# A two-layer encoder trunk in split fp32: the high and low parts of the stationary operands laid side by side

## The reference, cut to what matters

```python
for l in range(DEPTH):                                  # DEPTH = 2
    u = x @ (ev_w_in if l % 2 == 0 else od_w_in)[j]     # 2048 -> 6144 (6152) columns
    # layer 0: GLU -> causal depthwise conv (31 taps) -> LayerNorm -> silu | HGRN2, 8 heads, chunks of 64
    # layer 1: forgetting attention, 8 heads | chunked attention with a relative bias, 8 heads
    mix = concatenate([left, right], -1) @ w_out[j]     # 2048 -> 2048
    x = layer_norm(ALPHA * x + mix, ln_mix_g[l], ln_mix_b[l])
    h = square(relu(x @ mlp_w1[l])) @ mlp_w2[l]         # 2048 -> 8192 -> 2048
    x = layer_norm(ALPHA * x + h, ln_mlp_g[l], ln_mlp_b[l])
```

## Time and profile before

| | |
|---|---|
| median of the runs | 2276.03 us (2274.78 to 2277.2) |
| profiled execution | 2273.79 us, of which its span 2272.1 us |
| TensorE matmul busy | 2242.8 us, 99%, 10331 matmuls |
| TensorE weight load busy | 1858.2 us, 82%, 10331 loads |
| VectorE busy | 1341.5 us, 59% |
| ScalarE busy | 1056.6 us, 47% |
| DMA | 418.50 MB, 184 GB/s on average |
| granted TensorE clock | 0.998 of full |

### The profile page before, as it was taken

One profiled execution on the slowest core, in us unless ns is written; L12 is line 12 of the kernel. 1 busy time (PEld: TensorE's weight loads), 2 busy tenths in 40 slices (PEclk: granted clock), 3 DMA queues, 4 the chain that ended last, 5 costly groups with the idle time before them and its releaser, 6 DMA issues.

```text
span 2272.1 us, 28509 instructions
## 1 busy us (share of the span) xinstructions
PE 2242.8 (99%) x10331; PEld 1858.2 (82%) x10331; DVE 1341.5 (59%) x1472; ACT 1056.6 (47%) x1146; POOL 36.3 (2%) x68
## 2 busy tenths in 40 slices
PE   8999999999999999999999999999999999999998
PEld 7888778788888888888878888887888888888886
DVE  4898987855545444545565445568455454544455
ACT  4555565454354344444334444444544444443542
POOL 2000000000000001000000000000000000000000
PEclk9999999999999999999999999999999999999999
DMA  7555545565656656555636555575555565555553
GB/s 243 173 161 157 174 133 180 173 212 188 197 190 224 202 185 203 185 185 187 196 123 191 174 177 166 160 230 170 185 190 185 185 227 198 181 192 200 183 188 111
DMA packets 213040, 418.50 MB, mean 184 GB/s; under 512 B 12793, under 2 KB 13361, under 8 KB 211904
## 3 DMA queue, kind: packets, MB, share of 16 engines
q1 hardware_dynamic: 210832, 406.37, 55.7%
q0 software_dynamic: 1808, 10.04, 1.2%
q10 hardware_dynamic: 288, 0.52, 0.1%
HBM read 414.79 MB, written 2.10 MB: 183 GB/s over the span
## 4 chain that ended last, share of the span: by engine, by line
PE 91%; DVE 5%; issue 1%; ACT 1%; DMA 1%; SPq 0%; POOL 0%; DVEq 0%; ACTq 0%
PE gemm L1349 29%; PE gemm L1351 28%; PE gemm L1350 28%; DVE lnp L1091 1%; PE pair L1735 1%; DVE w_lo L811 1%; PE pair L1504 1%; ACT w_hi L495 1%; DMA raw<-in_ev_w_out 1%; PE pair L1421 1%; PE pair L1461 0%; DMA raw<-in_ev_w_in 0%; PE pair L1577 0%; PE pair L1649 0%; PE pair L1622 0%
## 5 line engine op out<-in xcount | busy, mean ns | idle before, releaser
L1222 DVE TENSOR_TENSOR w_lo<-raw,w_hi 128x1024 fp32r<-128x1024 f32 x488 | 596.7, 1225 | 482.0 <-ACT w_hi L719 452.2
L719 ACT ACTIVATE w_hi<-raw 128x1024 fp32r<-128x1024 f32 x492 | 521.9, 1061 | 629.3 <-PE gemm L1351 608.5
L1349 PE MATMUL gemm<-w_hi,x_hi 128*128 128x512 f32 x1792 | 708.7, 395 | 6.9 <-DVE w_lo L811 5.5
L1351 PE MATMUL gemm<-w_hi,x_lo 128*128 128x512 f32 x1792 | 699.0, 390 | 0.0
L1350 PE MATMUL gemm<-w_lo,x_hi 128*128 128x512 f32 x1792 | 698.3, 390 | 0.0
L1349 PE MATMUL gemm<-w_hi,c_hi 128*128 128x512 f32 x1280 | 501.0, 391 | 1.6 <-DVE X L839 1.0
L1351 PE MATMUL gemm<-w_hi,c_lo 128*128 128x512 f32 x1280 | 498.9, 390 | 0.0
L1350 PE MATMUL gemm<-w_lo,c_hi 128*128 128x512 f32 x1280 | 498.7, 390 | 0.0
L811 DVE TENSOR_TENSOR w_lo<-raw,w_hi 128x1024 fp32r<-128x1024 f32 x280 | 340.4, 1223 | 190.0 <-ACT w_hi L495 184.3
L495 ACT ACTIVATE w_hi<-raw 128x1024 fp32r<-128x1024 f32 x276 | 289.7, 1057 | 304.3 <-PE gemm L1351 266.0
L1349 PEld LDWEIGHTS gemm<-w_hi,x_hi 128*128 128x128 f32 x1792 | 337.0, 188 | 81.7 <-issue 5.4
(11 more groups left out here) (194 smaller groups left out, 798.4 us busy)
## 6 DMA issues: line engine op xcount, KB each, us to landing
raw<-in_mlp_w SPq DMA_DIRECT2D x512, 512.0 KB, 4.7
raw<-in_ev_w_in SPq DMA_DIRECT2D x96, 512.0 KB, 3.8
raw<-in_od_w_in SPq DMA_DIRECT2D x96, 512.0 KB, 4.0
raw<-in_ev_w_out SPq DMA_DIRECT2D x32, 512.0 KB, 4.1
raw<-in_od_w_out SPq DMA_DIRECT2D x32, 512.0 KB, 3.6
lnp<-in_ln_mix_g POOLq DMA_DIRECT2D x2, 1024.0 KB, 6.0
lnp<-in_ln_mix_b POOLq DMA_DIRECT2D x2, 1024.0 KB, 7.7
lnp<-in_ln_mlp_g POOLq DMA_DIRECT2D x2, 1024.0 KB, 7.6
```

The costliest lines, as they stand in the source:

```text
L719: act.activation(hi_of_chunk(s), raw[:, s % RING], ACT.Copy).then_inc(hi_ready, 1)
L1222: dve.tensor_tensor(lo_of_chunk(s), raw[:, s % RING], hi_of_chunk(s).bitcast(F32), ALU.subtract).then_inc(lo_ready, 1)
L1349: pe.matmul(acc[:, r, :], hi[:, k + c, rows], high, start=begin, stop=False)
L1351: return pe.matmul(acc[:, r, :], lo[:, k + c, rows], high, start=False, stop=end)
```

## The change

The two tiles of x become one tile with a last dimension of two, and so do the two of the output tiles' operand. `x_hi`, `x_lo`, `c_hi` and `c_lo` are views of every other element. All that reads or writes them is unchanged in text, and addresses with a step of two elements (8 bytes) where it had a step of one: the stationary operand of every gemm product, the moving operand of lines 1592 to 1594, ScalarE's writes of the high parts, VectorE's reads of the high parts and writes of the low parts. The size in SBUF is the same. The instructions and their order on each engine are the same, and the line numbers behind the change are higher by one.

```diff
-        x_hi = sb("x_hi", [P, KT, S], F32R)
-        x_lo = sb("x_lo", [P, KT, S], F32R)
-        c_hi = sb("c_hi", [P, KT, S], F32R)
-        c_lo = sb("c_lo", [P, KT, S], F32R)
+
+        x_parts = sb("x_parts", [P, KT, S, 2], F32R)
+        c_parts = sb("c_parts", [P, KT, S, 2], F32R)
+        x_hi, x_lo = x_parts[:, :, :, 0], x_parts[:, :, :, 1]
+        c_hi, c_lo = c_parts[:, :, :, 0], c_parts[:, :, :, 1]
```

## The result

The kernel after takes 2332.73 us (2331.57 to 2333.87, three runs) against 2276.03: ratio 1.0249, 95% interval 1.0226 to 1.0272, so 56.7 us slower. Its profiled span is 2331.0 us, 58.9 more than before. The forecast was 2276.2 us, and the range ended at 2298.

The account below looks back on a forecast made before the run. TensorE, 91% of the chain, was taken as the bound, with 9216 matmuls at 0.2267 us. All terms were zero but 0.2 us for ScalarE: 2273.79 + 0.2 = 2274.0, plus 2.2 to the runs' median, 2276.2 us; range 2272 to 2298.

Parts of the forecast that it names:

- (1): Gemm stationary operands: 9216 loads with a step of two stay covered by the 227 ns window; taken as zero.
- Rival B: Loads and the 48 forget-logit streams: the step doubles them, exposed outside the stream; 2296 us, 0.9% slower, chance 0.14.
- 0.21 us between two loads: First two loads behind the transposes: sign of a doubled load, against 0.11 us if unchanged.
- the chain's piece: Eight transposes in the chain, or the gemm after: 0.98 instead of 0.87 us would be a sign of a doubled load.
- a reason, not a proof: Gemm stream: loads take nothing measurable from it today, which doesn't prove that a load over twice the memory wouldn't.
- Rival C: Gemm stream: the load becomes the bound, or collides with the stream; slower by much, chance 0.21.
- C's main case: Gemm loads: interval above 227 ns becomes the bound; with three times the interval +900 us, about 3180 us.
- Its second case: Gemm stream: strided load collides with the moving operand, 13 ns more per matmul, +123 us, 2399 us.
- Step (2): The 48 forget-logit matmuls stream with the step: between zero and +5.1 us; taken as zero.
- (3): ScalarE's 74 writes of high parts: at most 0.09 us each for 1024 elements; 0.2 us taken on the path.
- (4): VectorE's subtractions with the step: zero.
- Step (5): Order, DMAs, semaphores and bytes in SBUF stay as they were: zero.

Follow-up runs that it names:

- one_short: Kernel before, MLP first product: middle of three matmuls streams 64 columns, load step varied by tile; three matmuls take 574 ns at step one, 580 at two.
- pad8: Kernel before with 8 unused elements (32 bytes) in front of x_hi and 120 behind c_lo, no step: 2329.01 us, ratio 1.023.
- blocks: Changed kernel with high and low parts sharing a tile as whole blocks of 256 tokens, without a step: 2275.67 us, ratio 0.9996 to the kernel before.
- pad64: Kernel before with 64 unused elements (256 bytes) in front of x_hi and 64 behind c_lo, no step: 2276.26 us, ratio 0.9999.

## Why the prediction was wrong

**The step that failed is (1), the zero for 9216 strided loads.** It stood for two claims. The first, that the load still fits in its window, held: 118 ns of 227 (`one_short`). Rival B's doubled load fell with it: of its signs, 0.21 us between two loads and 0.98 for the chain's piece, the trace has 0.12 and 0.87. The second, that a strided load leaves the stream's interval as it is, was wrong. With the strided load each interval is 6.6 ns longer, 52.9 us in all. I had argued it away by comparing a matmul that has a load beside it with the last one, which has none. That compares recorded lengths of 0.39 us, which are latencies, while the price sits in the interval: in `pad8` the record grew by 7 ns only together with 233.3. Even the last matmul of the kernel after, with no load beside it, is recorded longer:

```profile
2320.42 0.40 PE L1352 MATMUL gemm<-w_hi,c_parts 128*128 128x512 f32 x1
```

So its record doesn't isolate the load's effect at all. The sentence "a reason, not a proof" was right, and the zero had no better support than that. The row chosen as nearest is of VectorE, which is another reader with no second stream of TensorE beside it.

**Rival C's collision came nearest, at twice the size.** C's main case, a load that becomes the bound, did not occur. Its second case took the 13 ns that the stream has above its 213.3 as the price of a collision and came to 2399 us. Measured were 6.6 ns. Half of those 13 ns would have given 9216 x 6.5 = 60 us, close to the 56.7 measured, but no row supports the half, so that would have been luck. The reason that the prediction gave for a collision, a load spread over twice the memory, isn't the whole of it either: `pad8` pays the same 6.6 ns with loads of neighbouring elements. The prediction asked only about the step and never about the start.

**Step (2) failed in the choice.** The upper end, +5.1 us, was the right one: +5.4 measured. The sixteen matmuls of 64 columns in the earlier trace rows could not show a doubling, as the prediction said of them, and yet I took zero. The Trainium skill, SBUF — State Buffer, section "Door 1: The DMA port swizzle", wants two hits in a 16-byte line for full bandwidth, and a step of two has them. For the moving operand the trace disagrees: single elements and pairs, each with two hits a line, run at half speed (451 ns), and only groups of four are near the full rate (231.1 and 233.3). For the load's own length it nearly agrees: some 6 ns more at step two. It says nothing of load and stream together.

**Steps (3) and (4) held.** ScalarE's line 707 went from 1025 to 1089 ns, inside the bound, and TensorE doesn't wait for it; VectorE's line 1208 stayed at 1224. **Step (5) held**: order and bytes changed nothing, as `blocks` shows for the shared tile.

**What is shown and what isn't.** Shown, for fp32r streams of 512 columns: the interval depends on where the load starts and on where the stream starts, with a price of 3 to 7 ns; the kernel before stands at a favourable place, where a move of its stationary tiles by 256 bytes costs nothing and one by 32 bytes costs 6.6 ns a matmul; a load of 128 columns with a step of two costs 3 to 7 ns at each of the twelve starts tried. Streams of 256 columns, fp32r or plain float32, don't pay for the step; no run gives plain float32 512 columns a pass, or moves the start beside a short stream. The Trainium skill, TensorE: Matmul & The Clock Gate, section "Step-by-step: what each phase is for", gives TensorE two independent read ports, so that loading the next weights takes no bandwidth from the running matmul. In part the runs agree: with half or a quarter of the columns in two loads of three, no tile's interval is below 226.7 ns. But the interval isn't free of the load: to move only the load's start by 8 elements took it from 226.7 to 233.3 ns. Argued only: that the two reads meet in some part of the memory, in a rhythm set by their addresses. Open: why the favourable place is still 13 ns above 213.3, and why the same addresses give 226.7 ns on one side of a group of transposes and 233.4 on the other.

Of the 61 us by count 52.9 appeared. Most of the rest is in layer 0's input and output projections: their intervals between neighbouring matmuls grew by 4.8 us where the count gives 10.0. Of all the intervals 255 were longer than 235 ns before the change, set by something other than the stream, and together they became 3.8 us shorter; 88 of them lie in those projections.

## What to carry to other kernels

In a stream bound by TensorE the start addresses of stationary and moving operand are worth a check: 32 bytes of padding cost 2.3% here, and 256 bytes nothing. From a place that is known to be good, move either by multiples of 256 bytes (what is known here are distances within the memory map, not absolute addresses), and give neither a step. A strided moving fp32r operand costs twice its time unless the pieces are four elements, while a load with a step of two costs little by itself (some 6 ns) and lengthens the interval of the 512-column stream beside it. When a cost is repeated 9216 times and bounded by another engine's row, take the measured slack of the interval as the bound, not zero.

## What the runs showed of the hardware that was not expected

- An fp32r stream of 512 columns ran at 226.7 or 233.3 ns with nothing changed but a start address (`pad64`, `pad8`), at granted clocks of 0.996 and 0.997, with loads recorded at 188 or 189 ns in both. With a load 4 elements further both values stood in one tile, ahead of and behind eight transposes.
- A load's own cost, estimated from `one_short`, goes 112, 118, 178, 245, 265, 225 ns for steps 1, 2, 3, 4, 8, 16: sixteen is cheaper than eight.
- Streams of 256 columns show no price for a load of step two: 119.8 and 120.0 ns in fp32r, 216 ns a pass in plain float32 with either step.
- Short streams of 64 columns behind loads of step two and three, and the first of step four, ran at a granted clock of 0.50; the tile before them, the same streams with unit-step loads, had run at 1.00, and so had the first matmuls of step two. That the step is the reason isn't shown.
